# The last two column blocks of both channel mixers' second product with seven products in place of eight

## The reference, cut to what matters

```python
D_MODEL = 2048
SEQ = 256
FFN_DIM = 256 * ((8 * D_MODEL // 3 + 255) // 256)
...
def conv_ffn(x, w_in, conv_w, conv_b, w_out):
    S = x.shape[1]
    u = jnp.einsum('bsd,df->bsf', x, w_in)
    ...
    g, val = jnp.split(c, 2, axis=-1)
    return jnp.einsum('bsf,fd->bsd', jax.nn.gelu(g) * val, w_out)
...
        f = conv_ffn(h, ffn_w_in[i], ffn_conv_w[i], ffn_conv_b[i], ffn_w_out[i])
        h = layer_norm(DEEPNORM_ALPHA * h + f, ln_g[i, 1], ln_b[i, 1])
```

## Time and profile before

| what | value |
|---|---|
| median of three runs | 2567.71 us (2567.67 to 2568.49) |
| profiled execution | 2568.06 us |
| its span, first to last instruction | 2566.3 us |
| PE busy | 2552.7 us, 99% |
| DVE busy | 1697.4 us, 66% |
| ACT busy | 1235.3 us, 48% |
| transfers | 496.05 MB, mean 193 GB/s |
| PE's last matmul starts at | 2556.05 us |

### The profile page before, as it was taken

The page is one execution under the profiler, slowest core; times in us unless marked ns, Lnnn a source line. Parts: engine busy times, 40 slices in busy tenths (PEclk is TensorE's granted clock), DMA queues, the critical chain, the costliest instruction groups (busy, mean ns, idle before and its releaser), DMA issues.

```text
span 2566.3 us, 40343 instructions
## 1 busy us (share of the span) xinstructions
PE 2552.7 (99%) x14286; PEld 2227.7 (87%) x14286; DVE 1697.4 (66%) x1922; ACT 1235.3 (48%) x1383; POOL 15.9 (1%) x39
## 2 busy tenths in 40 slices
PE   9999999999999999999999999999999999999998
PEld 9999888888888888888888888888888888888887
DVE  6666667767666796565555555554766767678955
ACT  4444445555555554434444344433455555555532
POOL 0000000000000000000000000000000000000000
PEclk9999999999999999999999999999999999999999
DMA  7554574555555656655555555566555555556464
GB/s 280 178 172 164 181 251 145 196 192 196 196 192 192 207 219 210 217 177 182 180 180 178 185 180 179 185 212 199 171 193 187 197 193 196 196 193 224 175 230 153
DMA packets 142032, 496.05 MB, mean 193 GB/s; under 512 B 15616, under 2 KB 17920, under 8 KB 141952
## 3 DMA queue, kind: packets, MB, share of 16 engines
q1 hardware_dynamic: 133344, 481.22, 56.0%
q10 hardware_dynamic: 8608, 13.73, 1.6%
HBM read 492.80 MB, written 2.10 MB: 193 GB/s over the span
## 4 chain that ended last, share of the span: by engine, by line
PE 99%; DVE 0%; DMA 0%; SPq 0%; POOL 0%; issue 0%; ACT 0%; DVEq 0%; POOLq 0%; ACTq 0%
PE acc_cm L522 12%; PE acc_ab L522 11%; PE acc_ab L421 11%; PE acc_ab L420 11%; PE acc_ab L418 11%; PE acc_cm L525 6%; PE acc_ab L525 6%; PE acc_ab L435 4%; PE acc_ab L432 4%; PE acc_ab L434 4%; PE acc_cm L418 3%; PE acc_cm L421 3%; PE acc_cm L420 3%; PE acc_cm L688 1%; PE acc_cm L689 1%; PE acc_cm L687 1%
## 5 line engine op out<-in xcount | busy, mean ns | idle before, releaser
L1121 DVE TENSOR_TENSOR w_lo<-raw,w_hi 128x1024 fp32r<-128x1024 f32 x862 | 1045.4, 1223 | 678.3 <-ACT w_hi L797 673.0
L797 ACT ACTIVATE w_hi<-raw 128x1024 fp32r<-128x1024 f32 (+1 forms) x866 | 901.9, 1054 | 753.7 <-PE acc_ab L421 344.3
L522 PE MATMUL acc_cm<-x_parts,w_hi 128*128 128x512 f32 x1408 | 480.1, 389 | 0.0
L522 PE MATMUL acc_ab<-x_parts,w_hi 128*128 128x512 f32 x1280 | 436.2, 389 | 0.0
L525 PE MATMUL acc_cm<-x_parts,w_lo 128*128 128x256 f32 x1408 | 388.6, 276 | 0.0
L525 PE MATMUL acc_ab<-x_parts,w_lo 128*128 128x256 f32 x1280 | 353.3, 276 | 0.0
L522 PEld LDWEIGHTS acc_cm<-x_parts,w_hi 128*128 128x128 f32 x1408 | 264.3, 188 | 54.9
L432 PE MATMUL acc_ab<-x_parts,w_hi 128*128 128x256 f32 x1020 | 284.7, 279 | 1.3 <-DVE x_parts L1150 0.9
L522 PEld LDWEIGHTS acc_ab<-x_parts,w_hi 128*128 128x128 f32 x1280 | 240.2, 188 | 50.0
L435 PE MATMUL acc_ab<-x_parts,w_lo 128*128 128x256 f32 x1020 | 282.0, 276 | 0.0
L434 PE MATMUL acc_ab<-x_parts,w_hi 128*128 128x256 f32 x1020 | 282.0, 276 | 0.0
(11 more groups left out here) (199 smaller groups left out, 3251.1 us busy)
## 6 DMA issues: line engine op xcount, KB each, us to landing
raw<-in_weights_dram SPq DMA_DIRECT2D x878, 512.0 KB, 4.1
pair_raw<-in_weights_dram SPq DMA_DIRECT2D x32, 512.0 KB, 5.4
ln_gain<-in_ln_g_dram ACTq DMA_DIRECT2D x16, 256.0 KB, 5.0
ln_bias<-in_ln_b_dram ACTq DMA_DIRECT2D x16, 256.0 KB, 6.4
h<-in_x_dram ACTq DMA_DIRECT2D x4, 512.0 KB, 7.1
x_t<-in_x_by_feature_dram SPq DMA_DIRECT2D x7, 256.0 KB, 8.0
raw<-in_weights_dram SPq DMA_DIRECT2D x4, 256.0 KB, 4.9
decay_sb<-in_decay_tab_dram ACTq DMA_DIRECT2D x1, 1024.0 KB, 7.2
```

Source lines behind the costliest of these rows:

```text
L522: pe.matmul(acc[:, f], wh[:, k, c], x_parts[:, CK * s + k].rearrange("p a n -> p (a n)"), start=s == 0 and k == 0, stop=False, skip_group_ ...
L797: return act.activation(o, i, ACT.Copy)
L1121: dve.tensor_tensor(wl, raw[:, at % RING], wh.bitcast(F32), ALU.subtract).then_inc(lo_ready, 1)
```

## The change

Blocks 2 and 3 of each layer become a second pair, with four units of seven items and 28 plain chunks, so 56 positions where 44 chunks stood. Pairs are numbered 0 to 3, two for each layer, and all functions of the pair take the pair's number.

- The first unit starts at position 4 of pair 1 (layer 0) and at position 2 of pair 3 (layer 1); the distance between units stays at four plain chunks.
- Each unit of the new pairs loads its four chunks into `pair_raw` and makes four differences.
- `assembled(pair)` puts both pairs together; `residual` of block 2 goes, and block 3 is added unscaled since `add_p5_p6_p1` has scaled it.
- The LayerNorm parameters share their memory with `pair_raw`. They now load after the last unit has been read: from step 41 of pair 1 and step 39 of pair 3, again two in every second step.
- The four early chunks begin at position 46 (pair 1) and 42 (pair 3) of 56; in layer 1 they lie over the hidden tokens, since `x_parts` is in use. `last_product` starts at chunk 48.

```diff
+UNITS = 4
 ITEMS = 7
-LEAD = [12, 16, 20, 24]
-UNIT_AT = [LEAD[u] + ITEMS * u for u in range(UNITS_OUT)]
...
+LEAD = [[12, 16, 20, 24], [4, 8, 12, 16], [12, 16, 20, 24], [2, 6, 10, 14]]
+UNIT_AT = [[at + ITEMS * u for u, at in enumerate(lead)] for lead in LEAD]
+UNIT_AFTER = [at[-1] + ITEMS - 1 for at in UNIT_AT]
+PAIR_EARLY = [None, PAIR - 10, None, PAIR - RING - 10]
...
-EARLY_FROM = [None, (Q_WO + 2 * XQ, XCH), (Q_OUT0 + OQ0, HCH + 12), (Q_RWO + 3 * RQ, RCH - 2 * RING),
-              (Q_OUT1 + OQ0, HCH + 6)]
-LAST_CHUNK = [None, 2 * XCH, 2 * HCH, RCH, 2 * HCH - RING]
+EARLY_FROM = [None, (Q_WO + 2 * XQ, XCH), (Q_OUT0 + PQ, PAIR_EARLY[1]), (Q_RWO + 3 * RQ, RCH - 2 * RING),
+              (Q_OUT1 + PQ, PAIR_EARLY[3])]
+LAST_CHUNK = [None, 2 * XCH, PAIR, RCH, PAIR - RING]
...
-                 early_views(3, 0, 2 * part), early_views(4, 0, word * RING * CHUNK, x_parts_at)]
+                 early_views(3, 0, 2 * part), early_views(4, 0, word * FT * SEQ)]
...
+                pair_stream(second, q_out + PQ, LAST_CHUNK[stage] - RING,
+                            merged({UNIT_AFTER[second]: [copy_p1]}, ln_slots(stage, UNIT_AT[second][-1] + T4 + 1)),
+                            pair_early_slots(stage))
...
+                        at = position(s + RING, early_at)
+                        item = stage_item(layer, PAIR * (pair % 2) + at)
+                        if item is not None:
+                            later = at >= PAIR
+                            split_item(pair + later, turn + PQ * later, *item)
...
+                pair_stream(first, q_out, PAIR, merged(behind_value(FSTEPS - 1), assembled(first), {
+                    PAIR - 1: [add_second_block]}), {4 + u: [lambda u=u: low_sums(u)] for u in range(UNITS)})
+                pair_stream(second, q_out + PQ, LAST_CHUNK[stage] - RING, assembled(second), early_slots(stage, 0))
```

More of the change, by code:

```diff
@@ L103, in item_of, with plain_of, stage_item, skipped @@
     return None
[L106 to L116, removed]
+def plain_of(pair, i):
+    n, p = divmod(i - ITEMS * sum(at + ITEMS <= i for at in UNIT_AT[pair]), PLAIN_BLOCK)
+    return n, 2 * UNITS + p
+def stage_item(layer, i):
+    for pair in (2 * layer, 2 * layer + 1):
+        at = i - PAIR * (pair % 2)
+        if 0 <= at and item_of(pair, at) is not None:
+            return item_of(pair, at)
+    return None
+def skipped(layer, i):
+    return sum(stage_item(layer, j) is not None for j in range(i % RING, i, RING))
+def loaded_before(layer, i):
     j = i - RING
-    while j >= 0 and item_of(j) is not None:
+    while j >= 0 and stage_item(layer, j) is not None:
         j -= RING
@@ new lines, in pair_product @@
+                    last.then_inc(products, counts(i))
+                if held is not None:
+                    for i in range(chunks, PAIR):
+                        pe.wait_ge(lo_ready, count(i))
+                        done = plain_tile(i, 0)
+                    done.then_inc(first_tile, 1)
+                    for i in range(chunks, PAIR):
+                        plain_tile(i, 1).then_inc(products, counts(i))
+                        for step in held.get(PAIR - i, ()):
+                            step()
@@ L1560, in pair_stream @@
+                def pair_stream(pair, turn, chunks, slots, behind):
+                    early_at = PAIR_EARLY[pair]
+                    for s in range(chunks):
+                        dve.wait_ge(products, RING * turn + position(s, early_at) + 1)
                         for step in slots.get(s, ()):
                             step()
-                        if item_of(s + RING) is not None:
-                            split_item(*item_of(s + RING))
+                        at = position(s + RING, early_at)
+                        item = stage_item(layer, PAIR * (pair % 2) + at)
+                        if item is not None:
+                            later = at >= PAIR
+                            split_item(pair + later, turn + PQ * later, *item)
@@ L1725, in weight_stream @@
     parts += with_early(rwo, 3, w_in[1][0]) + up(1)
[L1726 to L1728 removed]
+    first, second = paired(w_out[1], 1)
+    held = PAIR - 2 * RING
+    parts += with_early([first, second[:held], second[held + RING:]], 4, second[held:held + RING])
     return np.ascontiguousarray(np.concatenate(parts, axis=0))
```

330 lines of the change are left out of this document (172 added, 158 removed).

## The result

The changed kernel took **2575.2 us** (median of 8 runs, 2573.4 to 2576.1) against 2568.0 us for the kernel before on the same chip (8 runs, 2567.7 to 2568.8). The ratio is 1.0027, with a 95% interval of 1.0018 to 1.0036: 7 us slower, where the forecast was no change and the range ended at 2574. The profiled execution took 2574.2 us, 2572.0 of it in the span, which is 5.7 us more than the span of before (2566.3).

A forecast was written before the change was run, and what follows sets the result against it. PE was taken to bound the kernel, busy 99% of the span. Fewer matmuls (-10.9) plus waits at three places (2.8, 5.6, 2.0) gave -0.5 us against the profiled 2568.06, so 2567.2 against the median 2567.71; range 2561 to 2574.

The forecast's parts named there:

- What is removed: Both layers: 24 matmuls less in each, 48 x 0.2267 = 10.9 us off PE, all on the path.
- Place 1: Between the pairs, layer 1: pair 3's first differences delay DVE's splits; 2.8 us of waiting (2.0 to 3.2).
- Place 2: End of layer 1: PE waits for the fourth early chunk behind DVE's work and late loads; 5.6 us (2.9 to 6.9).
- the 1 to 3 us that were to show it: Sign in the profile after: ACT waits for `raw` by 1 to 3 us in the steps with parameter loads.
- Place 3: End of layer 0: the same meeting as at layer 1's end, milder; PE waits 2.0 us, the middle of 0 to 3.7.
- The sum: Whole kernel, against the profiled execution: -10.9 + 2.8 + 5.6 + 2.0 = -0.5 us, forecast 2567.2 us.
- rival (d): PE's clock falls in the gap at layer 1's end: +3.9 - 0.5, 2571.1 us; chance 0.05.
- Rival (c): Both layer ends: loads of `raw` land at 6.9 us, each early chunk passing lateness on; +7.6, 2575.3 us; chance 0.12.
- The sum of the waits: Sign over the whole kernel: the prediction falls if PE's waits sum to less than 5 or more than 16 us.
- Load pressure: Steps with parameter loads: 8.4 MB in 21.8 us, 385 GB/s, what the queues can do, so some slips.

The follow-up runs named there:

- all edits: Changed kernel with early chunks spread, units of both second pairs at leads 4, 8, 11, 14, and parameter loads early by SP: 2557.24 us, ratio 0.9958.
- fillers: Changed kernel with 14 more matmuls of 512 columns in layer 1's last product, ahead of the wait for the early chunks: 2573.6 us.
- one chunk ahead: Changed kernel with the first of four early chunks of each second pair moved between two units, before chunk 24 (pair 3) and 26 (pair 1): 2567.3 us.
- parameters early: Changed kernel with the eight parameter loads of each end issued by SP instead of ACT, and earlier: 2568.0 us.
- by SP late: Changed kernel with the parameter loads issued by SP instead of ACT, at about the changed kernel's time: 2571.5 us.

## Why the prediction was wrong

**What is removed** was right: 48 matmuls, all on the path. The kernel with all edits gives back 10.7 of the 10.9 us.

**Place 1** was right in kind and size: 2.8 us forecast, 2.9 measured, three gaps of 1.0, 0.8 and 0.8 us beyond the usual distance, and it vanishes with the unit two positions later. No wait came between the pairs in layer 0, as the prediction said.

**Place 2**, the waiting, was nearly right in size and wrong in shape: 5.6 forecast, 2.5 + 3.8 = 6.3 measured, within the upper end of 6.9. (By the prediction's own terms the ends come out at 2.7 and, with a landing of 6.9 in the last sum, 7.5; the difference changes nothing here.) ACT's waits for `raw` were longer than the 1 to 3 us that were to show it, up to 4.4. The prediction had one wait of PE, ahead of the first `early_hi` matmul. ACT's and DVE's timelines show why there is one more before it:

```profile
2519.19 1.06 ACT L831 ACTIVATE w_hi<-raw 128x1024 fp32r<-128x1024 f32 x1 [3.23 <-DMA raw<-in_weights_dram]
2521.76 1.06 ACT L831 ACTIVATE early_hi<-raw 128x1024 fp32r<-128x1024 f32 x1 [1.51 <-DMA raw<-in_weights_dram]
...
2522.85 1.22 DVE L1182 TENSOR_TENSOR early_lo<-raw,early_hi 128x1024 fp32r<-128x1024 f32 x1 [1.34 <-ACT early_hi L831]
2523.99 1.22 DVE L1562 SCALAR_TENSOR_TENSOR h<-h,acc_cm 128x1024 f32<-128x1024 f32 x1
...
2526.33 1.22 DVE L1164 TENSOR_TENSOR w_lo<-raw,w_hi 128x1024 fp32r<-128x1024 f32 x1
```

The second early chunk came late (its load took 6.8 us in the chain), DVE's list has it and three sums of the assembly ahead of the split of a plain chunk that PE needs first, and the sums alone hold that split back by 2.2 us. With the sums later this first gap was 0.4 us.

**Place 3** was the first step that failed: 2.0 forecast from bounds of 0 and 3.7, 4.5 measured. The mechanism was the one named, late loads beside the parameter loads; the term was mis-sized. The bound was set with 1.5 us of slack on PE's side and one late load carried through. The chain above carries three, one behind the other, with 3.9 us of DVE's sums between the first two, and the last four chunks are wanted every 1.36 us, so that lateness is not made up there. With the parameter loads out or earlier, the place costs 1.6 to 1.7, near the 2.0 of the forecast: what was priced comes to the case without the meeting that the prediction had described.

**The clock** was the second. The sum held nothing for it, and rival (d) gave it one chance in twenty, with a note that nothing in the trace says a gap of this length suffices. It fell twice, 3.5 us together. (d) had one fall for 3.9 us, priced from the start of the kernel, where the low level lasts longer than the 3 us seen here. The price of one was twice too large, the chance far too small: in each of the eight kernels here that had waits of 2.5 to 6.1 us at place 2 the clock fell. The Trainium skill, "TensorE: Matmul & The Clock Gate", section "What's actually happening", says that an idle array falls back to the lower level; the traces agree, as the windows at 0.83 behind the gaps of 2.5 and 3.8 us show, and the one at 1.00 where fillers stood in the gap.

The two together, 4.5 - 2.0 = 2.5 and 3.5, with 0.7 for place 2, are 6.7 of the 6.8 us between the forecast's 10.4 us of losses and the 17.2 measured. Forecast and median are 8.0 us apart, 2567.2 and 2575.2; of the 1.2 us that this leaves, 1.0 is that the profiled execution was quicker than the median one. **Rival (c)**, loads falling behind, was the right mechanism: 2575.3 against 2575.2. Its time was right by luck. It put 10.3 us into place 2 as waiting, where 6.3 was waiting and 3.5 the clock, it had place 3 at 5.4 for 4.5, and its condition, loads landing at 6.9 us, was met by the slowest only; the median was 5.3. The fault in the working was to add a wait and leave out what it entails, the clock, and to take each chance on its own, while places 2 and 3 both grew with the same late loads. The sum of the waits, 13.7 us, stayed inside the 5 to 16 in which the prediction said it would stand; with them alone the time would have been some 2571, inside the range. The slow matmuls took it out.

**Load pressure** was argued rightly. The loads of `raw` rose from a median of 4.4 to 5.3 us. The Trainium skill, "DMA: Bandwidth & Descriptors", section "Issuing engines are not separate DMA queues", says that transfers run on the same 16 DMA engines and interleave, whichever engine started them. The runs agree at layer 0's end: the gaps there are 3.9 us with ACT as the issuer and 4.0 with SP as the issuer at nearly the same time, and 1.4 with SP earlier.

## What to carry to other kernels

When a change moves work into a stretch where loads, rounding and splits go round a small ring, ask how many steps of that ring in a row will find their load late, since each hands its lateness to the next. Two remedies worked here. Spreading the extra chunks over the whole stream, with the units moved a little, gave back 16 of the 17 us (2.9 of them at place 1, by the units' move) though the loads stayed as late. And where that can't be done, look for a stretch next to it where the queues stand idle (here the last unit's own items) and for transfers that may go there; moving them gave back 7. And a wait of PE has a second price, the matmuls at the lower clock behind it: put it into the sum as soon as a wait of some microseconds stands there. In the changed kernel it was 1.8 us for each of the waits of 2.5 and 3.8 us.

## What the runs showed of the hardware

When PE had stood still for 2.4 to 3.8 us it started again at the full clock, fell to the lower level 0.3 to 1.9 us later, and stayed there for some 3 us of steady matmuls, 0.43 us each. It did so behind gaps of 2.5 and 3.8 us (changed kernel), 2.6 (one chunk ahead) and 2.9 (no parameter loads, parameters early, by SP late, and the first gap with the fillers), and not behind the one of 1.9 us in layer 0 of the changed kernel. Behind the gaps of 6.1 us (sums later) and 6.0 us (units later) the lower level was there at once: the first two starts are 0.6 us apart and the next 0.43. A gap of 2.4 us in layer 0 went both ways. In the kernel with the fillers the clock did not fall behind it. In the kernel with the parameters by SP late it fell, 0.3 us after the restart; there PE had stood idle for another 1.6 us just before, with 1.5 us of work between. Its window, with PEclk at 0.79:

```profile
1093.00:1101.00 8.00, 7.50 (x26) 6.05 (x27) 4.36 (x7) 1.56 (x3) 0.93 (x2) 0.79 0.59 181
```

The times of the changed kernel spread over 2.7 us in 8 runs, those of the kernel before over 1.1 and those of the kernel with all edits over 0.5. A kernel whose PE waits for loads at a few places has an uncertain time; the widest spread, 5.4 us, is that of the kernel without the parameter loads.
